# The first units of a hybrid encoder layer: adaLN columns and alpha/beta made in four 32-column groups of the array

## The chip, the core and the metric

The kernel runs on one core of one Trainium2 chip. A core has five instruction streams that run side by side and meet through semaphores: TensorE (matmul; PE in the profile, with its weight loads as PEld), VectorE (DVE), ScalarE (ACT), GpSimd (POOL) and SyncE (SP), the last of which here only issues transfers (DMA) between device memory and the core's own memory. The metric is the device time of one execution in microseconds (us); lower is better.

## The reference, cut to what matters

One layer on a sequence of 1024 rows of width 1024. What the change touches is the front of it: the modulation that all of the input norm hangs on, and eight of the columns of the combined input projection.

```python
cond = jax.nn.silu(c)
mod = (cond @ w_ada[l] + b_ada[l])[:, None, :]
sh1, sc1, gt1, sh2, sc2, gt2 = jnp.split(mod, N_MOD, axis=-1)
h = rmsnorm(x, norm1_g[l]) * (1.0 + sc1) + sh1
proj = h @ w_in[l]
qa, ka, va, qkvb, zb, bb, ab, ga, gb = jnp.split(proj, IN_SPLITS, axis=-1)
...
beta = jax.nn.sigmoid(b_raw.astype(jnp.float32))
g = -jnp.exp(a_log.astype(jnp.float32)) * jax.nn.softplus(
    a_raw.astype(jnp.float32) + dt_bias.astype(jnp.float32))
```

`bb` and `ab` (four heads each) are the eight columns that this text calls alpha/beta. Behind them come a gated DeltaNet on `qkvb`, a chunked attention, a merge, and a feed-forward part that takes the larger half of the time.

## The kernel before, in words

Activations lie transposed: 128 of the 1024 channels on the partitions, the 1024 rows of the sequence along them, so a 1024-wide operand is eight tiles (k = 0 to 7). The order of everything is written out by hand, one program for each engine; nothing is scheduled by a tool.

A dense unit `ds` makes 128 output columns of a projection. Each operand is split into a high and a low part (`act_hi`, `act_lo`, `w_hi`, `w_lo`), and `dense_k` (L1189) issues for one k three products of two halves of 512 rows each, six matmuls of 128x512 in the fast fp32r format, into the PSUM pair `ps[ds % 2]`. Plain fp32 matmuls are also used; each shows as two records.

The start of the layer, which is where the change lies, goes like this.

- SP loads the small vectors, the first adaLN weights (`load_ada(0)`), the eight row tiles of x (tile t >= 4 waits until tile t-4 is transposed, since four places are shared), `load_ada(1)`, the weights of unit 0 and unit 1, three small vectors, `load_ada(2)`, `load_ada(3)`, the weights of units 2 to 5. Then come two stores: `xT_d` (L631, the transposed x, 4 MB) and `ext_d` (L633, a table of eight rows of 384 numbers, each written 128 times, 1.5 MB), and then the weights of units 6 to 8, each when its place in `w_raw` is free.
- TensorE transposes x, and for each of four pieces n of the modulation (256 shift and 256 scale columns) runs `modulation(n)`: 12 matmuls of 128x128 for the last three k, and 4 on a sum that VectorE has made of the first five (`ada_sum`, five instructions of 128x512). `beat` is filler work. `units01(n)` runs units 0 and 1 together, two k at a time, as soon as the low part of each k is there.
- Unit 0 is the alpha/beta unit: 128 columns from `C_AB` on are multiplied, of which eight are used (L1786). Unit 1 is the first of the twelve convolution units.
- VectorE and ScalarE turn x into `act_hi` and `act_lo`, two k for each piece n, once `mod_mm` says that the piece's columns are in PSUM.

From unit 1 on, a convolution unit d goes: matmuls on TensorE; ScalarE copies `ps` into `est[d % 2]` (L1776) and splits the weights of unit d+2; VectorE makes `w_lo` of d+2, adds three shifted taps (L2268), ScalarE a tanh, VectorE the product (L2273, `est_ready`); GpSimd issues the store to `qkvb_d` (L1050). Two rules tie this chain together: unit d+2 may not write `ps[d % 2]` before `est_ready` of d, and the copy of unit d into `est[d % 2]` waits until the store of unit d-2 has landed (`est_stored`, in `evac_conv`). The first such wait is that of unit 3 on the store of unit 1.

## Time and profile before

| | |
|---|---|
| median of three runs | 1651.31 us (1647.7 to 1651.38) |
| the profiled execution | 1652.54 us |
| its span | 1649.9 us |
| TensorE busy | 1608.8 us, 98% of the span |
| VectorE, ScalarE, GpSimd busy | 927.8, 638.9, 266.0 us |
| first step of units 0 and 1 | 43.5 us |
| first step of unit 2 | 72.55 us |
| first step of unit 5 | 107.33 us |

The page of the profile shows how full each engine is over the whole span. It says little on a change to the first 70 us: there the instructions in order of time, with the idle time ahead of each and its releaser in square brackets, are what is read. A busy share that is near 100% only says that work taken off TensorE may shorten the span; whether it does is decided by the next wait that does not depend on TensorE.

### The profile page before, as it was taken

What the parts mean: (1) busy time and instruction counts of PE and PEld (TensorE: products, weight loads), DVE (VectorE), ACT (ScalarE), POOL (GpSimd) and SP (SyncE); (2) the same over time, 40 slices, a digit from 0 to 9 for tenths busy, and PEclk for the clock granted to TensorE, in tenths of its full rate; (3) what the DMA queues carried; (4) which work ended last, traced back from release to release, by engine and by line L of the source; (5) the groups of instructions that cost most, each with busy time, mean ns of one, the idle gap of its engine ahead of it and who ended that gap; (6) DMA issues with size and microseconds to landing.
All of it is one profiled execution on the core that took longest, in us unless ns stands there. A gap on an engine that the chain in (4) does not pass through costs nothing.

```text
span 1649.9 us, 24004 instructions
## 1 busy us (share of the span) xinstructions
PE 1608.8 (98%) x8235; PEld 1328.9 (81%) x8235; DVE 927.8 (56%) x1459; ACT 638.9 (39%) x1308; POOL 266.0 (16%) x283
## 2 busy tenths in 40 slices
PE   5999999999999999999899999999999999999998
PEld 5877878888878787878788877888888888888887
DVE  5867665445444444545553399866666666334424
ACT  4234456555534444444212235333333333332413
POOL 1016580111110101100000012322332220000000
PEclk9999999999999999999999999999999999999999
DMA  9835657655833333422546312222222223643412
GB/s 296 221 104 191 223 170 227 183 178 153 250 101 106 103 108 97 132 101 99 171 148 203 102 53 77 97 84 87 76 76 76 95 75 138 216 177 130 145 45 102
DMA packets 223652, 223.42 MB, mean 135 GB/s; under 512 B 18025, under 2 KB 189162, under 8 KB 223594
## 3 DMA queue, kind: packets, MB, share of 16 engines
q1 hardware_dynamic: 216618, 197.50, 38.0%
q0 software_dynamic: 6976, 25.17, 4.0%
q8 instruction: 33, 0.54, 0.1%
q14 instruction: 25, 0.20, 0.0%
HBM read 162.35 MB, written 60.29 MB: 135 GB/s over the span
## 4 chain that ended last, share of the span: by engine, by line
PE 81%; DVE 4%; DMA 1%; ACT 1%; issue 0%; DVEq 0%; SPq 0%; ACTq 0%
PE pm L1595 22%; PE pm L1609 15%; PE pd L1454 11%; PE ps L1194 11%; PE pm L1194 9%; PE sc L1407 2%; PE tT L1430 2%; PE tT L1419 2%; PE pm L1507 1%; PE gps L1344 1%; DMA gst<-z_d 1%; PE pm L1549 1%; PE gps L1357 1%; PE gps L1378 1%; PE gps L1371 1%; PE gps L1364 1%
## 5 line engine op out<-in xcount | busy, mean ns | idle before, releaser
L1194 PE MATMUL ps<-act_hi,w_hi 128*128 128x512 f32 x464 | 154.4, 414 | 5.3 <-DVE est L2273 2.8
L2167 DVE TENSOR_TENSOR w_lo<-w_raw,w_hi 128x1024 fp32r<-128x1024 f32 x61 | 78.6, 1289 | 125.1 <-ACT w_hi L1701 115.6
L1194 PE MATMUL ps<-act_lo,w_hi 128*128 128x512 f32 x464 | 143.7, 391 | 0.0
L1194 PE MATMUL ps<-act_hi,w_lo 128*128 128x512 f32 x464 | 143.4, 390 | 0.0
L1609 PE MATMUL pm<-act_hi,w_hi 128*128 128x512 f32 x352 | 137.2, 390 | 0.0
L1609 PE MATMUL pm<-act_hi,w_lo 128*128 128x512 f32 x352 | 137.0, 389 | 0.0
L1609 PE MATMUL pm<-act_lo,w_hi 128*128 128x512 f32 x352 | 136.9, 389 | 0.0
L1595 PE MATMUL pm<-act_hi,w_hi 128*128 128x512 f32 x320 | 124.5, 389 | 0.0
L1595 PE MATMUL pm<-act_lo,w_hi 128*128 128x512 f32 x320 | 124.5, 389 | 0.0
L1595 PE MATMUL pm<-act_hi,w_lo 128*128 128x512 f32 x320 | 124.5, 389 | 0.0
L1454 PE MATMUL pd<-act_hi,w_hi 128*128 128x512 f32 x256 | 111.3, 435 | 0.0
L1194 PEld LDWEIGHTS ps<-act_lo,w_hi 128*128 128x128 f32 x464 | 87.1, 188 | 19.1
L1194 PEld LDWEIGHTS ps<-act_hi,w_lo 128*128 128x128 f32 x464 | 87.1, 188 | 19.0
L1454 PE MATMUL pd<-act_hi,w_lo 128*128 128x512 f32 x256 | 101.0, 394 | 0.0
L1454 PE MATMUL pd<-act_lo,w_hi 128*128 128x512 f32 x256 | 100.3, 392 | 0.0
L1194 PEld LDWEIGHTS ps<-act_hi,w_hi 128*128 128x128 f32 x464 | 80.8, 189 | 21.4 <-issue 9.0
L1595 PE MATMUL pm<-t_hi,w_hi 128*128 128x512 f32 x240 | 93.6, 390 | 3.3 <-DVE tmp L2638 3.3
L2744 DVE TENSOR_TENSOR w_lo<-w_raw,w_hi 128x512 fp32r<-128x512 f32 x44 | 30.4, 692 | 117.0 <-ACT w_hi L2069 116.9
L1170 POOL TENSOR_TENSOR est<-w_raw 128x512 f32<-128x512 f32 x20 | 27.1, 1353 | 418.8 <-DVE w_lo L2618 227.7
L1595 PE MATMUL pm<-t_hi,w_lo 128*128 128x512 f32 x240 | 93.4, 389 | 0.0
L1595 PE MATMUL pm<-t_lo,w_hi 128*128 128x512 f32 x240 | 93.4, 389 | 0.0
L1701 ACT ACTIVATE w_hi<-w_raw 128x1024 fp32r<-128x1024 f32 x61 | 64.4, 1056 | 60.2 <-PE pm L1194 53.1
(367 smaller groups left out, 3452.4 us busy)
## 6 DMA issues: line engine op xcount, KB each, us to landing
w_raw<-in_w_in_dram SPq DMA_DIRECT2D x45, 512.0 KB, 5.6
w_raw<-in_w_ffn_in_dram SPq DMA_DIRECT2D x44, 512.0 KB, 3.7
h_raw<-h_d SPq DMA_DIRECT2D x36, 512.0 KB, 3.4
a_raw<-in_w_ada_dram SPq DMA_DIRECT2D x32, 512.0 KB, 4.5
w_raw<-in_w_ffn_out_dram SPq DMA_DIRECT2D x44, 256.0 KB, 3.7
h_d<-hid SPq DMA_DIRECT2D x21, 512.0 KB, 2.6
pk_d<-pk SPq DMA_DIRECT2D x8, 768.0 KB, 3.7
qkva_d<-est POOLq DMA_DIRECT2D x12, 512.0 KB, 6.3
```

Of the source, the lines that this page charges most:

```text
L1170: pool.tensor_tensor(s1, upw[:, 0:4], upw[:, 4:8], ALU.add).then_inc(mix_ready, 1)
L1194: ins = pe.matmul(dst[:, cols], wt[:, ds % 2, k, :], at[:, cols], start=(first and n == 0), stop=(last and n == 2))
L1344: ins = pe.matmul(hd(gps, h), gst[:, (0 if q == Q_QS else 4) + h, :], hd(St, h), start=True, stop=True)
L1407: ins = pe.matmul(score_cols(e, c0, c1), ast[rows, 0, j * P:(j + 1) * P], ast[rows, 1, k0 + c0:k0 + c1], start=True, stop=True)
L1419: ins = pe.transpose(tT[:, kt * P:(kt + 1) * P], Pm[:, e, kt * P:(kt + 1) * P], ident[:, :])
L1430: ins = pe.matmul(tT[rows, 0:P], V[:, j - nk_ + 1 + kt, rows], PT[:, e, kt * P:(kt + 1) * P], start=(kt == 0), stop=(kt == nk_ - 1))
L1454: ins = pe.matmul(pd[:, half(h)], wt[:, ds % 2, kk, :], at[:, kk, half(h)], start=(kk == 0 and n == 0), stop=(kk == KT - 1 and n == 2))
L1595: ins = pe.matmul(bank(n, o), wt[:, c, :], at, start=(c == 0 and x == 0), stop=(c == 3 and x == 2))
L1609: ins = pe.matmul(out_bank(b, h), wt[:, b, :], at[:, j % 8, half(h)], start=(t % NF == 0 and x == 0), stop=(t % NF == NF - 1 and x == 2))
L1701: act.activation(w_hi[:, ds % 2], w_raw[:, ds % NR], ACT.Copy).then_inc(whi_ready, 1)
L2167: dve.tensor_tensor(w_lo[:, ds % 2], w_raw[:, ds % NR], w_hi[:, ds % 2].bitcast(F32), ALU.subtract)\
L2744: dve.tensor_tensor(lo, w_raw[:, raw_o(t) % NR, 0:4], hi.bitcast(F32), ALU.subtract)\
```

## The change

Four things are changed, all in the first units.

1. The modulation pieces. `modulation(n)` and VectorE's `ada_sum(n)` go. `columns(n)` is eight fp32 matmuls of 32x512 on TensorE: the stationary operand is one column of silu(c) repeated 32 times, the moving operand a row block of the adaLN weights, and k goes to the 32-column group k % 4 of the array, that is to partitions 32(k % 4) and on of `aT`. ScalarE copies `aT` to `asum` (`copy_columns`), and `turn_columns(n)`, four matmuls of 128x128, adds the four groups through `sel[:, 0]`, which is 1 at partitions 0, 32, 64 and 96. `mod_mm` counts two for a piece now.
2. Alpha/beta. Unit 0 goes, and with it its weights' place in `w_raw`. 32 columns of `w_in` lie in a tile of their own, `wab`. `ab_block(k)`, at odd k, runs eight fp32 matmuls of 32x512: for two k, for `act_hi` and `act_lo`, for both halves; the four (k, operand) pairs go to the four groups. ScalarE copies all 128 partitions of `ps[0]`, and the transposes become products with `sel`, which add the groups.
3. The order. `columns(0)` stands between the transposes of x tiles 2 and 3, `turn_columns(0)` behind tile 5; SP loads `wab` and unit 1 ahead of `load_ada(1)`; ScalarE and VectorE split unit 1's weights before the first norm; unit 2's weights may be split without waiting for a unit.
4. GpSimd makes `sel` with three small additions.

```diff
+        sel = sb("sel", [P, 2 * B_H])
...
+            wab = sbin(st0, "wab", [P, KT, 32])
...
         ACT_X = (3, 6)
+        AB_COLS = 32
...
                 load_x(t)
+            sp.dma_start(wab[:, :, :], w_in_v[:, :, C_AB:C_AB + AB_COLS]).then_inc(misc_in, 16)
+            sp.sem_inc(raw_in[0], 16)
+            load_unit(1, 0, w_in_v, C_QKVB + group(1) * P)
             load_ada(1)
-            for d in range(2):
-                load_unit(d, 0, w_in_v, C_AB if d == 0 else C_QKVB + group(1) * P)
             sp.dma_start(rrow[:, :], rel_rev).then_inc(rel_in, 16)
...
+            pool.wait_ge(consts_ready, 3)
+            ch.link(pool.tensor_tensor(sel[:, :], ident[:, 0:8], ident[:, AB_COLS:AB_COLS + 8], ALU.add))
+            ch.link(pool.tensor_tensor(sel[:, :], sel[:, :], ident[:, 2 * AB_COLS:2 * AB_COLS + 8], ALU.add))
+            pool.tensor_tensor(sel[:, :], sel[:, :], ident[:, 3 * AB_COLS:3 * AB_COLS + 8], ALU.add)\
+                .then_inc(consts_ready, 1)
             for n, b in enumerate((BLK, 2 * BLK)):
...
-            def units01(n):
-                for d, k in in_step(2 * n, 2 * n + 2):
-                    if d == 0:
-                        pe.wait_ge(lo_ready, k + 1)
-                    ins = dense_k(d, k, ps[d], act_hi[:, k, :], act_lo[:, k, :], k == 0, k == 7)
-                    if k == 7:
-                        ins.then_inc(dense_mm, 1)
+            def ab_block(k):
+                if k == 1:
+                    pe.wait_ge(misc_in, 48)
+                for b in (k - 1, k):
+                    for x, at in enumerate((act_hi, act_lo)):
+                        for h in range(2):
+                            c = 2 * b + x
+                            rows = slice(c % 4 * AB_COLS, (c % 4 + 1) * AB_COLS)
+                            ins = pe.matmul(ps[0][rows, half(h)], wab[:, b, :], at[:, b, half(h)].bitcast(F32),
+                                            start=(c < 4), stop=(c >= 2 * KT - 4))
+                if k == KT - 1:
+                    ins.then_inc(dense_mm, 1)
+            def units01(k):
+                pe.wait_ge(lo_ready, k + 1)
+                if k % 2:
+                    ab_block(k)
+                ins = dense_k(1, k, ps[1], act_hi[:, k, :], act_lo[:, k, :], k == 0, k == KT - 1)
+                if k == KT - 1:
+                    ins.then_inc(dense_mm, 1)
...
+            def columns(n):
+                pe.wait_ge(ada_in[n], ada_count(n))
+                if n:
+                    pe.wait_ge(asum_ready, n)
+                for k in range(KT):
+                    ins = pe.matmul(aT[k % 4 * AB_COLS:(k % 4 + 1) * AB_COLS, :],
+                                    cs[:, k:k + 1].broadcast_to([P, AB_COLS]), ada_row(n, k),
+                                    start=(k < 4), stop=(k >= 4))
+                ins.then_inc(mod_mm, 1)
+            def turn_columns(n):
+                pe.wait_ge(asum_ready, n + 1)
+                if n:
+                    pe.wait_ge(mod_ready, n)
+                for q in range(4):
+                    ins = pe.matmul(gps[:, q * P:(q + 1) * P], asum[:, n % 2, q * P:(q + 1) * P],
+                                    sel[:, 0:1].broadcast_to([P, P]), start=True, stop=True)
+                ins.then_inc(mod_mm, 1)
...
-            def modulation(n):
...
-            pe.wait_ge(cs_ready, 1)
-            pe.wait_ge(vecT_ready, 2)
-            modulation(0)
-            beat(12)
+                if t == 2:
+                    pe.wait_ge(cs_ready, 1)
+                    columns(0)
+                if t == 5:
+                    pe.wait_ge(vecT_ready, 2)
+                    pe.wait_ge(consts_ready, 4)
+                    turn_columns(0)
+            beat(8)
             pe.wait_ge(diag_ready, 1)
...
             ins.then_inc(rb_mm, 1)
-            modulation(1)
+            columns(1)
+            turn_columns(1)
+            pe.wait_ge(xt_read, NT)
             beat(8)
-            pe.wait_ge(xt_read, NT)
             pe.wait_ge(wlo_ready, 2)
             units01(0)
-            modulation(2)
+            columns(2)
             units01(1)
-            modulation(3)
+            turn_columns(2)
             units01(2)
             units01(3)
+            columns(3)
+            units01(4)
+            turn_columns(3)
+            for k in (5, 6, 7):
+                units01(k)
             for d in range(2, D_CONV):
...
                     pe.wait_ge(mod_ready, 1)
+                    pe.wait_ge(consts_ready, 4)
                     for t in range(NT):
-                        ins = pe.transpose(gps[:, t * 8:(t + 1) * 8], est[0:8, 0, t * P:(t + 1) * P],
-                                           ident[0:8, 0:8])
+                        ins = pe.matmul(gps[:, t * 8:(t + 1) * 8], est[:, 0, t * P:(t + 1) * P], sel[:, :],
+                                        start=True, stop=True)
                     ins.then_inc(abT_mm, 1)
...
                 act.wait_ge(raw_in[ds % NR], raw_count(ds, i))
-                if ds >= 2:
+                if ds >= 3:
                     act.wait_ge(dense_mm, ds - 1 + 4 * i)
...
             act.activation(ngh[:, :], vT[:, V_NG:V_NG + 1], ACT.Copy, scale=0.5).then_inc(act_chain, 1)
+            def copy_columns(n):
+                act.wait_ge(mod_mm, 2 * n + 1)
+                act.activation(asum[:, n % 2, :], aT[:, :], ACT.Copy).then_inc(asum_ready, 1)
             for t in range(NT):
+                if t == 5:
+                    copy_columns(0)
                 act.wait_ge(xr_in[t % 4], 16 * (t // 4 + 1))
...
                                    ACT.Copy).then_inc(xt_read, 1)
-            act.wait_ge(misc_in, 32)
+            act.sem_inc(whi_ready, 1)
+            split_hi(1)
+            act.wait_ge(misc_in, 48)
             act.activation(negA[:, :], negA[:, :], ACT.Exp).then_inc(act_chain, 1)
-            for n in range(4):
-                for k in (2 * n, 2 * n + 1):
-                    act.wait_ge(xn_ready, k + 1)
-                    act.activation(act_hi[:, k, :], est[:, k % 2, :], ACT.Identity,
-                                   bias=modT[:, SH1 + k:SH1 + k + 1]).then_inc(hi_ready, 1)
-                    if n == 0:
-                        split_hi(k)
+            copy_columns(1)
+            for k in range(KT):
+                if k == 3:
+                    copy_columns(2)
+                if k == 5:
+                    copy_columns(3)
+                act.wait_ge(xn_ready, k + 1)
+                act.activation(act_hi[:, k, :], est[:, k % 2, :], ACT.Identity,
+                               bias=modT[:, SH1 + k:SH1 + k + 1]).then_inc(hi_ready, 1)
...
                     act.wait_ge(lo_ready, KT)
-                    act.activation(est[0:8, 0, :], ps[0][0:8, :], ACT.Copy).then_inc(ab_read, 1)
+                    act.wait_ge(dense_mm, 1)
+                    act.activation(est[:, 0, :], ps[0][:, :], ACT.Copy).then_inc(ab_read, 1)
                     continue
...
-            def ada_sum(n):
...
-            ada_sum(0)
             for t in range(NT):
...
             dve.wait_ge(xt_read, NT)
-            ada_sum(1)
+            dve.wait_ge(whi_ready, 1)
+            dve.sem_inc(wlo_ready, 1)
+            split_lo(1)
...
             for n in range(4):
-                if n in (1, 2):
-                    ada_sum(n + 1)
-                dve.wait_ge(mod_mm, n + 1)
+                dve.wait_ge(mod_mm, 2 * n + 2)
                 two = slice(2 * n, 2 * n + 2)
...
                     norm_scale(k, xT0[:, k, :], gs[:, k:k + 1], aS[:, :], 0)
-                if n == 0:
-                    split_lo(0)
-                    split_lo(1)
                 for k in (2 * n, 2 * n + 1):
...
                     dve.wait_ge(abT_mm, 1)
-                    dve.wait_ge(misc_in, 32)
+                    dve.wait_ge(misc_in, 48)
                     ch.link(dve.tensor_copy(ab[:, :, :], gps[:, 0:64].rearrange("p (t h) -> p t h", t=NT)))
...
```

On TensorE the first steps of the units change most. Before, with the buffers' numbers (`ps0` is unit 0, `ps1` unit 1), the first k, in which unit 0 comes ahead of unit 1:

```order
L1194 MATMUL ps0<-act_hi,w_hi 128x512 [waits lo_ready,wlo_ready,xt_read]
L1194 MATMUL ps0<-act_hi,w_hi 128x512
L1194 MATMUL ps0<-act_lo,w_hi 128x512 x2
L1194 MATMUL ps0<-act_hi,w_lo 128x512 x2
L1194 MATMUL ps1<-act_hi,w_hi 128x512 x2
```

and now, from the same place on, up to the end of the second k:

```order
L1203 MATMUL ps1<-act_hi,w_hi 128x512 [waits lo_ready,wlo_ready]
L1203 MATMUL ps1<-act_hi,w_hi 128x512
L1203 MATMUL ps1<-act_lo,w_hi 128x512 x2
L1203 MATMUL ps1<-act_hi,w_lo 128x512 x2
L1259 MATMUL aT<-ada_raw,cs 32x512 [waits asum_ready,ada_in2]
L1259 MATMUL aT<-ada_raw,cs 32x512 x7
L1234 MATMUL ps0<-act_hi,wab 32x512 [waits misc_in,lo_ready]
L1234 MATMUL ps0<-act_hi,wab 32x512
L1234 MATMUL ps0<-act_lo,wab 32x512 x2
L1234 MATMUL ps0<-act_hi,wab 32x512 x2
L1234 MATMUL ps0<-act_lo,wab 32x512 x2
```

Unit 0's six matmuls of each k have become eight of 32x512 for every two k, and the piece's columns stand behind the first k.

On ScalarE, from the last square of x on (`tmp,ss<-xr`) to the copy of alpha/beta, before:

```order
L1713 ACTIVATE tmp,ss<-xr 128x1024 [waits ss_ready,xr_in3]
L1721 ACTIVATE negA<-negA 128x4 [waits misc_in]
L1725 ACTIVATE act_hi<-est,modT 128x1024 [waits xn_ready]
L1701 ACTIVATE w_hi<-w_raw 128x1024 [waits raw_in0]
L1725 ACTIVATE act_hi<-est,modT 128x1024 [waits xn_ready]
L1701 ACTIVATE w_hi<-w_raw 128x1024 [waits raw_in1]
L1725 ACTIVATE act_hi<-est,modT 128x1024 [waits xn_ready] x6
L1701 ACTIVATE w_hi<-w_raw 128x1024 [waits dense_mm,raw_in2]
L1786 ACTIVATE est<-ps 8x1024 [waits lo_ready]
```

and now:

```order
L1762 ACTIVATE tmp,ss<-xr 128x1024 [waits ss_ready,xr_in3]
L1743 ACTIVATE w_hi<-w_raw 128x1024 [waits raw_in1]
L1772 ACTIVATE negA<-negA 128x4 [waits misc_in]
L1754 ACTIVATE asum<-aT 128x512 [waits mod_mm]
L1780 ACTIVATE act_hi<-est,modT 128x1024 [waits xn_ready] x3
L1754 ACTIVATE asum<-aT 128x512 [waits mod_mm]
L1780 ACTIVATE act_hi<-est,modT 128x1024 [waits xn_ready] x2
L1754 ACTIVATE asum<-aT 128x512 [waits mod_mm]
L1780 ACTIVATE act_hi<-est,modT 128x1024 [waits xn_ready] x3
L1743 ACTIVATE w_hi<-w_raw 128x1024 [waits raw_in2]
L1840 ACTIVATE est<-ps 128x1024 [waits dense_mm,lo_ready]
```

Three copies of `aT` stand between the `act_hi` now (the first, of piece 0, stands ahead of the square of tile 5), and unit 2's weights wait for no unit.

On SyncE the transfers from the late x tiles on, before:

```order
L580 DMA xr<-in_x_dram 128x1024 [waits xt_mm,ss_ready] x4
L586 DMA adab<-in_w_ada_dram 128x8x256 x2
L566 DMA w_raw<-in_w_in_dram 128x8x128 x2
L596 DMA rrow<-in_rel_table_dram 8x257
L597 DMA negA<-in_a_log_dram 128x4
```

and now:

```order
L583 DMA xr<-in_x_dram 128x1024 [waits xt_mm,ss_ready] x4
L596 DMA wab<-in_w_in_dram 128x8x32
L569 DMA w_raw<-in_w_in_dram 128x8x128
L589 DMA adab<-in_w_ada_dram 128x8x256 x2
L600 DMA rrow<-in_rel_table_dram 8x257
```

A quarter of one unit's bytes has taken the place of that unit, and what follows down to `ext_d` and units 6 to 8 is as it was.

## Rows read from the trace of the kernel before

**Rows 1.** Timeline, TensorE: start us, us, engine, line, operation, tiles, shapes, count [idle before].
```profile
43.52 0.47 PE L1194 MATMUL ps<-act_hi,w_hi 128*128 128x512 f32 x1 [2.49 <-DVE act_lo L2217]
...
49.05 0.83 PE L1247 MATMUL gps<-cs,ada_raw 128*128 128x128 f32 x6
...
52.54 0.71 PE L1194 MATMUL ps<-act_hi,w_hi 128*128 128x512 f32 x2
...
72.55 0.64 PE L1194 MATMUL ps<-act_hi,w_hi 128*128 128x512 f32 x2
...
105.62 0.61 PE L1194 MATMUL ps<-act_hi,w_lo 128*128 128x512 f32 x2
107.33 0.70 PE L1194 MATMUL ps<-act_hi,w_hi 128*128 128x512 f32 x2 [1.10 <-DVE est L2273]
```

**Rows 2.** Timeline, ScalarE and VectorE, unit 3's evacuation and its last step.
```profile
97.69 1.12 ACT L1776 ACTIVATE est<-ps,wcT 128x1024 f32<-128x1024 f32 x1 [5.21 <-DMA qkvb_d<-est]
...
105.96 1.22 DVE L2273 SCALAR_TENSOR_TENSOR est<-tmp,est 128x1024 f32<-128x1024 f32 x1 [1.13 <-ACT tmp L1780]
```

**Rows 3.** Timeline, the queues of SP and POOL: when transfers are issued.
```profile
14.84 4.53 SPq L580 DMA_DIRECT2D xr<-in_x_dram  x4
...
48.37 1.74 SPq L631 DMA_DIRECT2D xT_d<-xT  x1
50.15 1.78 SPq L633 DMA_DIRECT2D ext_d<-ext  x1
...
82.56 0.77 POOL L1050 DMA_DIRECT2D qkvb_d<-est  x1 [47.16 <-DVE est L2273]
```

**Rows 4.** The tile qkvb_d, window 82 to 84: unit 1's store.
```profile
DMA to landing us min/median/max: 15.0/15.0/15.0
```

**Rows 5.** DMA queues in 82.5:86, 86:93.5, 94:98: packets, MB, share of 16 engines.
```profile
q0 software_dynamic: 72, 0.26, 18.3%
...
q1 hardware_dynamic: 762, 0.62, 57.6%
...
q0 software_dynamic: 154, 0.57, 43.2%
```

**Rows 6.** Stretches: us, TensorE busy (instructions), granted clock, DMA share, GB/s.
```profile
31.00:49.00 18.00, 14.60 (x104) 1.00 1.09 321
55.00:62.00 7.00, 7.00 (x49) 1.00 1.02 422
65.00:72.00 7.00, 7.00 (x32) 1.00 0.45 48
...
792.50:796.00 3.50, 3.23 (x8) 0.51 0.90 321
```

**Rows 7.** Timeline, TensorE, 128x64 products in two column groups; first row from window 467.36:467.50.
```profile
467.37 0.33 PE L1430 MATMUL tT<-PT,V 128*64 128x128 f32 x2
...
519.15 1.31 PE L1430 MATMUL tT<-PT,V 128*64 128x128 f32 x20
520.40 0.50 PE L1454 MATMUL pd<-act_hi,w_hi 128*128 128x512 f32 x1
```

**Rows 8.** Timeline, TensorE, windows 122.4:122.89 and 122.89:122.92: an fp32 matmul's two records.
```profile
122.47 0.59 PE L1293 MATMUL aT<-gm,after 128*128 128x512 f32 x1
...
122.47 1.02 PE L1293 MATMUL aT<-gm,after 128*128 128x512 f32 x2
```

**Rows 9.** Timeline, TensorE, behind long idle times, and the same transposes later.
```profile
12.79 1.97 PE L1234 MATMUL ps<-ident,xr 128*128 128x128 f32 x8 [7.86 <-DMA xr<-in_x_dram]
...
22.60 1.09 PE L1234 MATMUL ps<-ident,xr 128*128 128x128 f32 x8 [0.73 <-DMA xr<-in_x_dram]
...
792.77 1.22 PE L1194 MATMUL pm<-y_hi,w_hi 128*128 128x512 f32 x2 [4.37 <-DVE y_lo L2464]
```

**Rows 10.** Waits of TensorE up to 145 us: total, times, longest.
```profile
PE gps L1293 <- DVE pk L2260: 1.1, 1, 1.1
PE gps L1293 <- POOL gm L1060: 0.9, 1, 0.9
```

More of the change, by code:

```diff
@@ L1227, in _, with beat @@
             pe.transpose(gps[:, 0:n], vrow[:, :], ident[0:n, 0:n]).then_inc(vecT_mm, 1)
+            def columns(n):
[15 more added lines that the diff above has]
+                ins.then_inc(mod_mm, 1)
+            def beat(count):
+                for _ in range(count):
+                    pe.matmul(aT[:, 0:P], ones[:, :], ident[:, :], start=True, stop=True)
             for t in range(NT):
@@ L1236, in _ @@
                 ins.then_inc(xt_mm, 1)
-            def modulation(n):
-                pe.wait_ge(ada_in[n], ada_count(n))
-                pe.wait_ge(asum_ready, n + 1)
-                if n:
-                    pe.wait_ge(mod_ready, n)
-                for q in range(4):
-                    dst = gps[:, q * P:(q + 1) * P]
-                    for k in range(5, KT):
-                        pe.matmul(dst, ada_row(n, k)[:, q * P:(q + 1) * P], cs[:, k:k + 1].broadcast_to([P, P]),
-                                  start=(k == 5), stop=False)
-                    ins = pe.matmul(dst, asum[:, n % 2, q * P:(q + 1) * P], ones[:, :], start=False, stop=True)
-                ins.then_inc(mod_mm, 1)
-            def beat(count):
-                for _ in range(count):
-                    pe.matmul(aT[:, 0:P], ones[:, :], ident[:, :], start=True, stop=True)
-            pe.wait_ge(cs_ready, 1)
-            pe.wait_ge(vecT_ready, 2)
-            modulation(0)
-            beat(12)
+                if t == 2:
[6 more added lines that the diff above has]
+            beat(8)
             pe.wait_ge(diag_ready, 1)
@@ L2180, in evac_x @@
                     .then_inc(xt_read, 1)
-            def ada_sum(n):
-                dve.wait_ge(ada_in[n], ada_count(n))
-                dst = asum[:, n % 2, :]
-                ch.link(dve.tensor_scalar(dst, ada_row(n, 0), cs[:, 0:1], None, ALU.mult))
-                for k in range(1, 5):
-                    ins = dve.scalar_tensor_tensor(dst, ada_row(n, k), cs[:, k:k + 1], dst, ALU.mult, ALU.add)
-                    if k < 4:
-                        ch.link(ins)
-                ins.then_inc(asum_ready, 1)
-            ada_sum(0)
             for t in range(NT):
```

## Prediction, made before the changed kernel was run

> **What bounds the kernel now.** I read TensorE's instructions in order of time first. It waits 2.49 us for the first `act_lo`, starts the units at 43.52, runs through to 105.62 (and some 0.45 more for the last pair), and idles 1.1 us until unit 5 starts at 107.33 [rows 1]. So between 43.5 and 106.1 TensorE is the bound: work taken off it moves everything up to there.
>
> Then I asked what holds unit 5. It needs unit 3's last step on VectorE, which starts at 105.96 and takes 1.22; that chain begins at 97.69 with ScalarE's copy of unit 3, which sat 5.21 us waiting for a transfer, the store of unit 1 [rows 2]. It was issued at 82.56 [rows 3] and landed 15.0 us later [rows 4]. From 97.69 to 107.33 runs a chain of 9.64 us (copy, split, three taps, tanh, product) that does not contain TensorE.
>
> Why did 0.5 MB take 15 us? The transfers are full up to the big store of x, at 1.09 and 1.02 of the engines' time; then, from 65 on, the share is 0.45 at 48 GB/s: this is `ext_d`, issued at 50.15 behind `xT_d` [rows 3, 6]. 1.5 MB at 48 GB/s are 32 us, from about 63 to 95. Of unit 1's store, 72 packets moved before 86, none from 86 to 93.5 (only q1 is listed there), and the rest after 94 [rows 5]. So the store ended because `ext_d` ended. The clock that starts unit 5 is the transfer queue, not TensorE, and TensorE is only 1.25 us early against it today.
>
> **The change part by part.**
>
> *The array groups.* A plain fp32 matmul is two records; at 512 columns the second starts 0.43 us behind the first [rows 8], where one record is listed up to 122.89 and two from there. If four column groups run side by side, eight such matmuls (16 records) take 4 x 0.43 = 1.72 us; one after another 16 x 0.43 = 6.9. The trace has two groups, not four: of the 128x64 products two records lie in the same 0.14 us at 467.37, with one duration of 0.33, and 20 records take 520.40 - 519.15 = 1.25 us [rows 7]. A 128x128 record alone costs 0.109 (a modulation, 32 records, takes 52.54 - 49.05 = 3.49 [rows 1]), so twenty in a row would be 2.18 and ten pairs 1.09. Two groups do run in parallel, with some 0.16 for entering and leaving. I take 1.72 + 0.2 = 1.9 for each block of eight, `columns` or `ab_block`; the ends are 1.7 and 6.9.
>
> By the Trainium skill (TensorE: Matmul & The Clock Gate, Part 3: Packing small matmuls) packed matmuls start and end strictly in program order. By that rule a pair in one group would hold back the next group; in rows 7 two neighbours in different groups start at once, which the order of a matmul's two records does not allow if both halves of the first come first. The rule is the third rival below.
>
> *TensorE between its first unit step and unit 2.* Now: 29.03 us (43.52 to 72.55) = 16 steps of 1.38 (24 pairs in 5.53 us up to 49.05 are four steps) and two modulations of 3.49 [rows 1]. After: 8 steps x 1.38 = 11.0; four `ab_block` and two `columns`, 6 x 1.9 = 11.4; two `turn_columns`, each four of the sixteen matmuls of a modulation, 2 x 0.87 = 1.7. Sum 24.1: 4.9 us less. The first step comes some 3 to 4 us earlier, since the sum of piece 1 leaves VectorE's way to the first norm, though `columns(0)` now holds up the transposes of x tile 3 by 1.9. Against it stands a new wait: `act_hi(5)` is queued on ScalarE behind the copy of piece 3, which waits for `columns(3)`, and `turn_columns(3)` stands ahead of k = 5 on TensorE; I allow 2 us. Unit 2 then starts at 72.55 - 4.9 - 3.5 + 2 = 66.2. Its weights no longer wait for a unit, and the copy of `ps[0]` is queued in front of nothing that is late. Units 2 to 4 take 33.5 as now, plus 0.6 because the eight `sel` products load 128 columns instead of 8. TensorE is done with unit 4 at 100.3 instead of 106.1: 5.8 us gained.
>
> *Off VectorE.* The four sums and one weight split go, the split of unit 1 moves ahead. VectorE is not the bound after 68, so this is worth only what it did for the start above.
>
> *What the gain meets.* Unit 5 still waits for `est_ready` of unit 3, at 107.3. TensorE idles about 7 us there in place of 1.25. The 5.8 us end in this wait. What counts is whether `ext_d` ends earlier. Two terms. First, SP moves 128 KB instead of 512 KB ahead of it: at 321 GB/s [rows 6] 0.38 MB is 1.2 us; if the small pieces of `wab` cost as much each as the larger ones, nothing. Between 0 and -1.2 I take -0.6. Second, x tile 7 may only be issued when tile 3 is transposed, now behind `columns(0)`: up to 1.9 later, in a queue that has tiles 5 and 6 in front of it (four x tiles from 14.84 on) [rows 3]. Between 0 and +1.9 I take +0.4. Sum -0.2 us, ends -1.2 and +1.9.
>
> *The clock.* Behind 4.37 us of idle TensorE the granted clock was 0.51 for 3.5 us, the 1.2 GHz level, and 792.77's pair took 1.22; behind 7.86 us the transposes took 1.97 for eight against 1.09 [rows 6, 9]. Seven idle us ahead of unit 5 will do the same: 3.5 to 5 us at half rate, 1.7 to 2.5 us lost in unit 5. Of that, the next two waits of TensorE take back 0.9 (for GpSimd's gates, made behind unit 4's store) and 1.1 (for VectorE's `pk`) [rows 10]: both hang on chains that start at unit 3's last step, on VectorE and GpSimd. I take all of it as absorbed; the bound is +0.7.
>
> *Sum.* -0.2 + 0 = -0.2 us. Against the profiled execution's 1652.54 that is 1652.3; against the median of 1651.31, 1651.1, and the latter is what I forecast, rounded to 1651.0. Its own range is -1.5 to +2.6 and the spread of the runs (3.7 us): 1647.5 to 1654.5.
>
> **The rivals.**
>
> 1. *The store of unit 1 does not hang on `ext_d` but takes its 15 us from the issue.* For it: its two halves landed on different engines, and the same chain would then move with TensorE. Against: nothing moved from 86 to 93.5. Unit 5 would start when TensorE is free, at 100.3: -7.0, 1644.3. By the Trainium skill (DMA: Bandwidth & Descriptors, Queues, rings and completion order) an engine takes turns between its queues packet by packet, which speaks for this rival; the trace shows the software queue standing still beside the other, so I give it little.
>
> 2. *The groups do not run side by side when there are four, or in fp32 with 32 columns.* Then the first unit steps cost 6.9 in seven blocks (four `ab_block`, `columns(1)` to `(3)`): 7 x 5.0 = +35, less the 7.0 of idle before unit 5 and the 2.0 behind it: +26, 1677. Rows 7 speak against it.
>
> 3. *Slower, from the order of starts.* In `ab_block` a group gets both halves of the sequence, four records, before the next group. If starts keep to program order, each next group begins with the last record of the one before: 13 x 0.43 = 5.6 instead of 1.72, and `columns`, two records per group, 9 x 0.43 = 3.9. That is 4 x 3.9 + 3 x 2.2 = 22 us more on TensorE; 7.0 of it lies in the idle time, 2.0 in the two waits behind: +13, 1664. It decides from about 1.2 us of excess per block on (7.0 over six blocks); below that the cover holds and the time is as forecast. The 128x64 products can't show it fully: they alternate groups after each matmul.
>
> 4. *The clock is not given back,* or x tile 7 delays the whole queue: +1.5 to +3, 1653 to 1654. This stays within the likeliest case's own range.
>
> **How the numbers follow.** A measurement of this kernel tells 0.3%, about 5 us, from no change. Forecast with rival 4: 0.82, all of it "same". Rival 1: 0.07, faster by more than 5. Rivals 2 and 3: 0.03 and 0.06, slower. Odds and ends beyond 5 us on the fast side 0.02. So faster 0.09, same 0.82, slower 0.09. The range has to hold eight in ten: 1646 to 1656 leaves out rivals 1, 2 and 3, together 0.16.
>
> **What would show it.** In the changed profile: (a) `columns` and `ab_block` at under 2.2 us each, with four records starting together; (b) unit 2 starting at 64 to 69; (c) ScalarE's copy of unit 3 waiting for `qkvb_d<-est` for more than 10 us, until 96 to 99, and the 48 GB/s stretch ending at 93 to 96 as now; (d) TensorE idle some 7 us ahead of unit 5, which starts at 106.5 to 109, with the granted clock at half behind it; (e) from 137 on all instructions within 2 us of where they are now. It is wrong if unit 5 starts before 104, because the store lands early, or after 111, because the blocks take over 3 us.

## The result: slower, and the profile after

| | before | changed |
|---|---|---|
| median | 1651.17 us (4 runs) | 1662.99 us (4 runs, 1661.9 to 1664.16) |
| ratio | | 1.0071, 95% interval [1.0059, 1.0083] |
| span of the profiled execution | 1649.9 us | 1661.3 us |

Every median here is over the fast executions of a kernel, which leaves out one, of 5713 us (the kernel with `t` moved by 32 bytes, below).

The change costs 11.4 us of span. The forecast was no change, 1651.0 in a range of 1646 to 1656, so it was wrong, and by a loss that none of its rivals had the mechanism of.

The front is not where it went. Here is TensorE in order of time in the changed kernel, to be read against [rows 1] (start us, us, engine, line, operation, tiles, shapes, count, idle before):

```profile
40.38 1.92 PE L1259 MATMUL aT<-ada_raw,cs 128*32 128x512 f32 x16
42.12 0.59 PE L1234 MATMUL ps<-act_hi,wab 128*32 128x512 f32 x1
42.12 0.62 PE L1234 MATMUL ps<-act_lo,wab 128*32 128x512 f32 x1
42.14 0.62 PE L1234 MATMUL ps<-act_hi,wab 128*32 128x512 f32 x1
42.15 0.62 PE L1234 MATMUL ps<-act_lo,wab 128*32 128x512 f32 x1
42.55 0.59 PE L1234 MATMUL ps<-act_hi,wab 128*32 128x512 f32 x1
...
43.98 0.50 PE L1203 MATMUL ps<-act_hi,w_hi 128*128 128x512 f32 x1
...
65.38 0.62 PE L1203 MATMUL ps<-act_hi,w_hi 128*128 128x512 f32 x2
...
99.43 0.61 PE L1203 MATMUL ps<-act_hi,w_lo 128*128 128x512 f32 x2
105.77 1.19 PE L1203 MATMUL ps<-act_hi,w_hi 128*128 128x512 f32 x2 [5.72 <-DVE est L2312]
106.76 1.05 PE L1203 MATMUL ps<-act_lo,w_hi 128*128 128x512 f32 x2
107.61 1.05 PE L1203 MATMUL ps<-act_hi,w_lo 128*128 128x512 f32 x2
...
111.02 0.76 PE L1203 MATMUL ps<-act_hi,w_hi 128*128 128x512 f32 x2
```

Four records start within 0.03 us and the next four 0.43 us later: the groups run side by side. A block of eight takes 43.98 - 42.12 = 1.86 us. Unit 2 starts at 65.38, TensorE is done with unit 4 at 100.0, and unit 5 then waits 5.7 us.

The wait is the one that the prediction names. The store of unit 1 is issued 7.2 us earlier than in [rows 3] and lands only 1.6 us earlier (at 96.0, not 97.6), and ScalarE's copy of unit 3 waits for it longer than in [rows 2] (GpSimd's queue, landing of that store, ScalarE):

```profile
75.39 0.77 POOL L1059 DMA_DIRECT2D qkvb_d<-est  x1 [41.66 <-DVE est L2312]
```

```profile
DMA to landing us min/median/max: 20.6/20.6/20.6
```

```profile
96.12 1.12 ACT L1829 ACTIVATE est<-ps,wcT 128x1024 f32<-128x1024 f32 x1 [9.72 <-DMA qkvb_d<-est]
```

Now the same matmuls, from the end of the program back, compared by their start in both kernels. The table is worked out from the start times of both traces:

| us in the kernel before | 137 | 413 | 797 | 865 | 1022 | 1396 | 1600 | end |
|---|---|---|---|---|---|---|---|---|
| changed minus before, us | -1.5 | -0.1 | -0.3 | +1.9 | +1.3 | +8.3 | +11.0 | +11.4 |

Up to 797 us nothing is lost. The whole loss comes after it, in code that the diff does not touch and without a wait: 2.2 us from 797 to 865, where TensorE multiplies `y` with `w_hi`, nothing from 865 to 1022, where it is mostly `act` with `w_hi`, and the rest from 1022 on. The stretches show it (us, TensorE busy with its instructions, PEld, DVE, ACT, POOL, granted clock, DMA share, GB/s); first the kernel before, then the changed one:

```profile
800.00:865.00 65.00, 65.00 (x289) 53.72 (x288) 40.23 (x35) 13.67 (x13) 0.00 (x0) 1.00 0.46 156
1070.00:1396.00 326.00, 326.00 (x1440) 269.95 (x1439) 220.11 (x310) 112.10 (x190) 81.85 (x60) 1.00 0.26 86
1400.00:1600.00 200.00, 200.00 (x884) 165.62 (x883) 74.82 (x81) 62.71 (x78) 0.00 (x0) 1.00 0.43 152
```

```profile
800.00:865.00 65.00, 65.00 (x281) 52.20 (x280) 39.57 (x33) 12.72 (x13) 0.00 (x0) 1.00 0.45 147
1070.00:1396.00 326.00, 326.00 (x1412) 264.82 (x1411) 213.59 (x304) 108.74 (x186) 81.92 (x60) 1.00 0.26 84
1400.00:1600.00 200.00, 200.00 (x872) 163.50 (x871) 77.70 (x85) 62.46 (x78) 0.00 (x0) 1.00 0.45 157
```

TensorE is busy throughout and the clock is full, but fewer matmuls go through: 1412 instead of 1440 in 326 us, 326 us / 1412 = 230.9 ns each instead of 226.4.

### The profile page after: what moved, and what is told of

It reads as the page before. It is cut to its first block, busy times and chain, and to the rows that moved or that the text cites. A ratio compares the mean times of both kernels' runs of the same rounds, so it can differ in the third digit from the quotient of the medians.

```text
span 1661.3 us, 23963 instructions
## 1 busy us (share of the span) xinstructions
PE 1619.2 (97%) x8219; PEld 1315.3 (79%) x8219; DVE 908.8 (55%) x1438; ACT 639.6 (39%) x1311; POOL 267.9 (16%) x286
## 4 chain that ended last, share of the span: by engine, by line
PE 86%; DVE 4%; DMA 4%; POOL 2%; issue 1%; ACT 1%; SPq 1%; DVEq 0%; POOLq 0%; ACTq 0%
PE pm L1637 21%; PE pm L1651 15%; PE ps L1203 13%; PE pd L1496 11%; PE pm L1203 9%; PE sc L1449 2%; PE tT L1472 2%; PE pm L1591 2%; PE tT L1461 2%; POOL Xi L1119 1%; PE pm L1549 1%; DMA qkvb_d<-est 1%; POOL pr L1117 1%; PE gps L1386 1%; DMA gst<-z_d 1%
## 5 line engine op out<-in xcount | busy, mean ns | idle before, releaser
L1203 PE MATMUL ps<-act_hi,w_hi 128*128 128x512 f32 x448 | 151.0, 418 | 7.8 <-DVE est L2312 7.3
L2221 DVE TENSOR_TENSOR w_lo<-w_raw,w_hi 128x1024 fp32r<-128x1024 f32 x60 | 74.2, 1236 | 128.3 <-ACT w_hi L1743 117.4
L1203 PE MATMUL ps<-act_hi,w_lo 128*128 128x512 f32 x448 | 139.9, 393 | 0.0
L1203 PE MATMUL ps<-act_lo,w_hi 128*128 128x512 f32 x448 | 139.8, 393 | 0.0
L1179 POOL TENSOR_TENSOR est<-w_raw 128x512 f32<-128x512 f32 x20 | 26.7, 1335 | 426.1 <-DVE w_lo L2657 233.5
L2045 ACT ACTIVATE w_hi<-w_raw 128x512 fp32r<-128x512 f32 x80 | 50.1, 630 | 96.1 <-PE pm L1637 96.1
```

The source lines that it names most:

```text
L1179: pool.tensor_tensor(s1, upw[:, 0:4], upw[:, 4:8], ALU.add).then_inc(mix_ready, 1)
L1203: ins = pe.matmul(dst[:, cols], wt[:, ds % 2, k, :], at[:, cols], start=(first and n == 0), stop=(last and n == 2))
L2045: act.activation(op_slot(o)[0], op_source(n, o), ACT.Copy).then_inc(whi_ready, 1)
L2221: dve.tensor_tensor(w_lo[:, ds % 2], w_raw[:, ds % NR], w_hi[:, ds % 2].bitcast(F32), ALU.subtract)\
```

## Theories for the 11 us

The diff has one line that reaches so far: `sel = sb("sel", ...)`, 32 bytes on each partition, is allocated ahead of most other tiles. `act_hi`, `act_lo`, `w_hi`, `w_lo` lie in front of it and stay. `y_hi`, `y_lo`, `t_hi`, `t_lo`, `w3_hi`, `w3_lo` and all other later tiles move by 32 bytes. In the kernel before, all these operands start at 128 modulo 256 (`act_hi` 16512, `w_hi` 98432, `y_hi` 132992, `t_hi` 165760, `w3_hi` 214912).

*Place*: the late matmuls are slower because of where their operands lie. *Front*: the new front carries through (its transfers, idle time, clock). *Move*: any new layout is slower.

**Four kernels on the addresses.**

```diff
 # e1_after_pad32, the changed kernel
         sel = sb("sel", [P, 2 * B_H])
+        pad = sb("pad", [P, 8])
 # e2_before_pad32, the kernel before
         after = sb("after", [P, P])
+        pad = sb("pad", [P, 8])
 # e3_before_pad64, the kernel before
+        pad = sb("pad", [P, 16])
 # e4_after_sel_late, the changed kernel
-        sel = sb("sel", [P, 2 * B_H])
...
             ext = sbin(st0, "ext", [A_H, EXT])
+            sel = sbin(st0, "sel", [P, 2 * B_H])
```

> The changed kernel with 32 more bytes per partition behind the new tile sel, so that every tile allocated behind it lies 64 bytes (not 32) from where it lay in the kernel before. Theory P (place): the 11.4 us come from operands of the late matmuls (y_hi, y_lo, t_hi, t_lo, w3_hi, w3_lo) that lie 32 bytes off a 64-byte boundary, and nothing from the new front. Then they go, and the time is that of the kernel before less the 1.3 us by which unit 5 and the start of the chain run ahead, minus what is absorbed: 1649.5 to 1651.5, and 512-column matmuls that read y_hi or t_hi start every 226.7 ns again. Theory F (front): the late stages are slower because of what the new front does (its DMA order, the idle time and the clock). Then nothing changes: 1662 to 1664. Theory M (any move): what counts is that tiles have moved at all. Then 1658 to 1664.

> The kernel before with an unused tile of 32 bytes per partition where the changed kernel has sel, and no other edit. Theory P: all of the loss without any of the change, 1651.2 + 11.5 = 1662.7 (1661 to 1664), with 512-column matmuls on y_hi at 233 ns and on t_hi at 232 ns from start to start. Theory F: 1651. Theory M: 1658 to 1664.

> The kernel before with an unused tile of 64 bytes per partition in the same place. Theory P: 1651.2 as before, since all operands lie on a 64-byte boundary; if the boundary that counts is one of 128 bytes, it is slow like the pad of 32. Theory M: slow, 1658 to 1664. Theory F: 1651, as for the pad of 32 (this run alone does not tell F from P).

> The changed kernel with sel allocated as the last tile of the first scope, whose room is given up before the late stages: every tile that is not in that scope has the address that it has in the kernel before. Theory P: as for the changed kernel with the 32 bytes more, 1649.5 to 1651.5. Theory F: 1662 to 1664. It differs from the first run of this call if a shift by 64 bytes also costs something (then this one alone is back at 1650 to 1651).

The ratios are the record's; they are not the quotients of the two medians.

| | median us | ratio to before (1650.02) |
|---|---|---|
| changed, 64 bytes in all | 1661.43 | 1.0068 [1.0052, 1.0083] |
| before, unused 32 bytes | 1664.05 | 1.0085 [1.0066, 1.0104] |
| before, unused 64 bytes | 1657.65 | 1.0054 [1.0037, 1.0071] |
| changed, `sel` in the first scope | 1651.98 | 1.0006 [0.9996, 1.0016] |

Thirty-two unused bytes cost all of it without any of the change, and the whole change without the move costs nothing. *Front* is dead. The stretches of the last kernel are back at the old count:

```profile
1070.00:1396.00 326.00, 326.00 (x1440) 270.04 (x1439) 220.49 (x312) 112.36 (x190) 81.83 (x60) 1.00 0.26 86
```

My bet on a 64-byte boundary was wrong: 64 bytes cost 9 us too (8.8 and 8.6 us from 797 to 1600 by the starts of the two traces).

**What has to agree with what.** In the changed kernel the seven products of the feed-forward loop differ. Products 0 and 1 multiply moved weights (`w3`) with unmoved `act`: 233 ns. Products 5 and 6, unmoved `w_hi` with moved `t`: 233.5. Product 2, moved `w3` with moved `t`, settles at 227 after five matmuls. That suggests that the two operands of a matmul must agree with each other, not with a boundary.

```diff
 # r1_all_operands_32, the kernel before
+        pad = sb("pad", [P, 8])
         with ExitStack() as st:
             ada_raw = sbin(st, "ada_raw", [P, 2, KT, S])
         act_hi = sb("act_hi", [P, KT, S], F32R)
 # dw3_only_w3_32, the kernel before
+            sbin(st3, "pad", [P, 8])
             w3_hi = sbin(st3, "w3_hi", [P, 3, 4, P], F32R)
 # dt_only_t_32, the kernel before
+            sbin(st3, "pad", [P, 8])
             t_hi = sbin(st3, "t_hi", [P, 3, 4, HALF], F32R)
...
+            sbin(st3, "pad2", [P, 24])
             w3_hi = sbin(st3, "w3_hi", [P, 3, 4, P], F32R)
 # m128_t_and_w3_128: one pad of 32 numbers ahead of t_hi; m256_t_and_w3_256: of 64
```

> The kernel before with an unused tile of 32 bytes per partition ahead of act_hi, so that every tile, weights and moving operands alike, lies 32 bytes further and none against another. Theory R (relative): a matmul is slow where its moving operand and its weights begin at different offsets within 128 bytes. In the changed kernel the products with weights in w3 and moving tiles in act start every 233 ns, those with weights in w_hi and moving tiles in t every 233.5 ns, but the one with both in moved tiles (w3 and t_hi) settles at 227 ns after five matmuls. Then this kernel has the time of the one before, 1649 to 1652. Theory A (absolute): a matmul is slow where an operand lies off a 128-byte boundary. Then every 512-column fp32r matmul goes from 227 to 233 ns or more, the 6500 or so of them add 6 ns each, and the time is 1685 to 1695.

> The kernel before with 32 unused bytes ahead of w3_hi, so that only w3_hi and w3_lo (the weights of three of the seven products, and of steps t % 7 = 0, 1, 2 of the last stage) lie 32 bytes off. Both theories: products 0 and 1 (240 matmuls each, 6.3 ns more) 3.0 us, the 456 matmuls of the last stage at 233 instead of 226.8 ns 2.8 us, products 3 to 6 unchanged at 226.7. They part at product 2, whose moving operand t_hi has not been moved here: R says that it is now slow too, 233 ns instead of the 229.3 it had in the changed kernel, 1.5 us, and the time is 1650.5 + 7.3 = 1658 (1656 to 1659). If its time is that of the changed kernel or less, R is wrong.

> The kernel before with 32 unused bytes ahead of t_hi and 96 ahead of w3_hi: t_hi and t_lo lie 32 bytes off, w3_hi and w3_lo 128 bytes further, which is no move within 128 bytes. R and A: products 5 and 6 (t against w_hi) at 233.5 ns as in the changed kernel, 3.2 us; products 0 and 1 and the last stage at 226.7, although w3 has moved by 128. Product 2 (t against w3) at 233, 1.5 us. Time 1650.5 + 4.7 = 1655 (1653.5 to 1656.5). If it is any move at all that costs, products 0, 1 and the last stage stay slow and it is over 1659.

> The kernel before with 128 unused bytes ahead of t_hi: t_hi, t_lo, w3_hi and w3_lo all lie 128 bytes further, nothing else. The last call said that a move of w3 by 128 bytes against act is slow too (product 0 and 1 at 233 ns), so what counts is at least the offset within 256 bytes. Theory R256 (slow where moving operand and weights begin at different offsets within 256 bytes): products 0 and 1 (w3 against act), 5 and 6 (t against w_hi) and steps 0 to 2 of the last stage at 233 ns, product 2 (both moved by 128) near 227 after its first five matmuls as in the changed kernel: 1650.5 + 9 = 1659.5 (1658 to 1661). Theory A128 is dead by this: it says 1650.5.

> The same with 256 bytes. R256: a move by 256 changes no offset within 256, so 1650.5 (1649 to 1652) and 226.7 ns everywhere. If a larger period counts (512 or more), it is slow like the move by 128, 1658 to 1661; against that speaks that in the kernel before w_hi (address 98432, 128 within 512) is used against t_hi (165760, 384 within 512) at full pace. If any move costs: also 1658 to 1661.

| moved against the kernel before | median us | ratio |
|---|---|---|
| everything by 32 bytes | 1650.44 (before 1651.75) | 0.9994 [0.9984, 1.0005] |
| `w3` by 32 | 1657.68 (1651.75) | 1.0042 [1.0025, 1.0059] |
| `t` by 32, `w3` by 128 | 1663.36 (1651.75) | 1.0082 [1.0062, 1.0103] |
| `t` and `w3` by 128 | 1661.8 (1652.13) | 1.0047 [1.0031, 1.0062] |
| `t` and `w3` by 256 | 1650.52 (1652.13) | 0.9991 [0.9982, 1.0000] |

The mean time from start to start, worked out from the starts in each trace (ns; 240 matmuls for each product; the last column is the last stage's steps with `w3` weights):

| product: weights, moving | 0, 1: w3, act | 2: w3, t | 3: w_hi, act | 4: w_hi, act | 5, 6: w_hi, t | last stage |
|---|---|---|---|---|---|---|
| before | 226.7 | 226.7 | 226.7 | 226.7 | 226.8 | 226.8 |
| changed (`t`, `w3` by 32) | 233.1 | 229.3 | 228.7 | 226.7 | 233.5 | 232.9 |
| everything by 32 | 226.7 | 226.7 | 226.7 | 226.7 | 226.7 | 226.8 |
| `w3` by 32 | 233.1 | 233.4 | 227.0 | 226.7 | 227.1 | 232.8 |
| `t` by 32, `w3` by 128 | 233.3 | 234.1 | 230.4 | 226.7 | 233.4 | 232.2 |
| `t` and `w3` by 128 | 233.2 | 228.6 | 227.0 | 226.7 | 233.0 | 232.3 |
| `t` and `w3` by 256 | 226.7 | 226.7 | 226.7 | 226.7 | 226.8 | 226.8 |

Moving everything is free: by the expectation above, an absolute boundary would have cost 35 us and more. *Move* falls with it, and with the last row. Moving one operand of a pair is slow at 32, 64 and 128 bytes and free at 256 (products 5 and 6 take 229 to 230 ns at 64, products 0 and 1 take 233); product 2 of `t` by 32, `w3` by 128, whose operands differ by 96, takes 234.1. Steps between, such as 192 bytes, were not tried. Moving both by the same amount is free but for the first matmuls. Product 3 of the changed kernel has only unmoved operands, and its first five matmuls still take 228 to 236 ns, although product 2 had settled at 226.7 from its sixth to its last but one. So going from a pair at one common offset to a pair at another costs a few matmuls too.

My expectation for `t` by 32 took 128 bytes for a whole period and was 8 us low; that miss gave the period. The next two kernels bear it out, the one at 128 bytes with 1661.8 where 1658 to 1661 was expected. Why the offset counts is not settled: the trace shows the pace, not the port.

## Where the gain of the front went

With the tiles in place the change gives 1650.9 to 1652.0 in three measurements, as predicted, though TensorE is done with unit 4 earlier than before, by 4.4 us in two of the three traces and 2.5 in the third (6.1 in the changed kernel). Two things were said to hold it: the store of unit 1 ends with `ext_d`, and the clock halves behind the wait. Each was taken away. The first edit stores the eight rows once, and copies them 128-fold from device memory later, behind the load of unit 6 (65.5 instead of 50.1 us).

```diff
 # x1_ext_16_engines (sel in the first scope), x2_before_ext_16 (the kernel before)
-                    sp.dma_start(ext_d.rearrange("h (p n) -> h p n", n=EXT),
-                                 ext[:, :].unsqueeze(1).broadcast_to([A_H, P, EXT])).then_inc(ext_stored, 16)
+                    sp.dma_start(ext_s, ext[:, :]).then_inc(ext_stored, 16)
+                if d == 6:
+                    sp.wait_ge(ext_stored, 16)
+                    sp.dma_start(ext_d.rearrange("h (p n) -> p h n", n=EXT),
+                                 bass.AP(ext_s.tensor, 0, [[0, P], [EXT, A_H], [1, EXT]])).then_inc(ext_stored, 16)
```

> The changed kernel with its tiles in place (sel in the first scope), and with the 1.5 MB of ext_d made in two steps: 12 KB of ext to a small tensor, then one broadcast from there with the 128 rows as its outer dimension, behind the load of unit 6. Theory S (the store of unit 1 stands behind ext_d, as the prediction has it): its store lands by 86 to 88 instead of 96, unit 5 starts when TensorE is done with unit 4, at 100 to 101 instead of 105.8, the granted clock does not halve, and 5.5 + 3 us are gained at 120. How much of it reaches the end was never seen: small gains at 120 (1 us) came through to the end, losses of 3 to 4 us by half. All of it: 1651.5 - 8.5 = 1643; half of it: 1647. Rival: unit 5 waits for something else than that store (est of unit 3 on VectorE, a load); then it starts at 105 as now, and the time is 1650 to 1652.

> The kernel before with the same two steps for ext_d. Theory S: TensorE comes out of unit 4 only at 106.1 there, and waits 1.1 us for est; so no more than that 1.1 us can be gained, 1649.5 to 1651. The gain of the new front (5.8 us at 100) is then to be had only with both edits: this run near 1650 and the one with both at 1643 to 1647. If this run gains as much as that one, the gain is of the transfer (other loads land earlier), not of the TensorE time saved.

With the new front 1646.25 us (1644.19 to 1646.38), ratio 0.9956 [0.9943, 0.9969]; with the old front 1650.82, ratio 0.9989 [0.9980, 0.9998]. Both as expected. The first is faster than both kernels. Its ScalarE:

```profile
91.51 1.12 ACT L1833 ACTIVATE est<-ps,wcT 128x1024 f32<-128x1024 f32 x1 [2.80 <-PE ps L1207]
```

Then the stretch behind the wait, in the changed kernel and in this one:

```profile
105.00:110.00 5.00, 4.23 (x10) 3.39 (x11) 4.49 (x18) 2.06 (x2) 0.53 (x1) 0.50 0.26 105
```

```profile
105.00:110.00 5.00, 5.00 (x24) 4.14 (x23) 4.51 (x4) 0.38 (x1) 0.00 (x0) 1.00 0.00 0
```

The copy of unit 3 now waits for TensorE, not for a transfer, and the clock is full where it was half. Its starts lie 6.2 us ahead of the kernel before at 137 us and 5.2 at the end. On the two forms of the transfer, the changed kernel first, then this one:

```profile
79.00:86.00 7.00, 7.00 (x32) 5.79 (x31) 4.98 (x4) 1.88 (x3) 0.00 (x0) 1.00 0.47 52
```

```profile
65.00:72.00 7.00, 7.00 (x37) 4.92 (x30) 2.02 (x3) 3.09 (x3) 0.00 (x0) 1.00 0.86 284
```

The old form held a share near 0.5 at some 50 GB/s. In the new row two weight loads run beside the copy. By the Trainium skill (DMA: Bandwidth & Descriptors, Why a DMA increments its semaphore by 16 and not by 1) a transfer is split over the largest number of engines, 16 at most, that divides the slowest dimension of both its sides: eight for eight rows, all for 128. The shares, 0.47 and 0.86, agree. The edit also changes the source and the place in the queue, and no run separates these from the number of engines; what it does show is that without the long transfer unit 1's store lands after 3.3 us and unit 5 doesn't wait.

**Filling the wait.** These three and their comparison ask what the half clock costs.

```diff
 # x4_beats_at_unit5 (sel in the first scope); x5_22_beats: beat(22)
+            beat(40)
             for d in range(D_CONV, D_A):
 # x3_beats_before_unit5: in the loop of units 2 to 4, which d == 5 never reaches
+                if d == 5:
+                    beat(40)
```

> The changed kernel with its tiles in place, and 40 matmuls of 128x128 fp32 without use (0.12 us each by the eleven that take 1.39 us at 38.78) in the 5.7 us in which TensorE waits ahead of unit 5. The wait for est stays, so unit 5 begins at 105.8 as before. Theory C (the time lost behind the wait is that of the half clock): the granted clock stays at 1.0 behind 105, the 3.4 us (6.8 us at half) are not lost, 120.2 comes 3 to 3.5 us earlier than in the kernel without them, and the time goes from 1652.0 to 1649 (1648 to 1650.5), since such early gains have come through to the end. Theory D (what is late behind the wait is the chain of stores and loads, not TensorE's pace): the clock stays but unit 6 waits longer, and the time is 1651.5 to 1652.5.

> The changed kernel with its tiles in place and 40 matmuls of 128x128 fp32 without use (0.12 us each, 5 us) between unit 4 and unit 5, in front of the wait for est. In the last call these stood in a loop that never reaches unit 5, so that run was the kernel without them a second time. Theory C: the granted clock stays at 1.0 behind 105, unit 5 still starts when est is there, the 3.4 us of the half clock are not lost, 120.2 comes about 3 us earlier against the start of unit 5, and the time goes from 1651.6 (the two runs without them) to 1648.5 (1647.5 to 1650). Theory D (unit 6 and what follows wait longer instead, the chain of stores is what is late): 1651 to 1652.5.

> As the last run with 22 instead of 40 matmuls without use. The last trace has 80 records in 9.09 us for 40 of them, so one takes 0.227 us (not 0.12) and the 40 held unit 5 up until 110.7, and its time still was 1649.8 against 1652.0 and 1651.2 without any. 22 take 5.0 us and end at about 105.5, before est comes. Theory C: unit 5 starts with est (105.8), clock 1.0, 120.2 comes 3 us earlier than without them, and the time is 2 to 3.5 us below that of the kernel without them in the same call: 1648.5 (1647 to 1650). Theory D: within 1 us of it.

> The changed kernel with its tiles in place and nothing else, for the third time, beside the one with 22 matmuls without use on the same chip: 1651.5 (1650.5 to 1652.5).

The first, 1651.21 us, ratio 1.0002 [0.9989, 1.0014], issued nothing new and only repeats the kernel with `sel` in the first scope. The second, 1649.8 us, ratio 0.9993 [0.9983, 1.0002], was mis-sized: I had read eleven records as eleven matmuls, and an fp32 matmul has two; it held unit 5 up until 110.71. The third, 1646.04 us, ratio 0.9979 [0.9968, 0.9991], against 1650.87, ratio 1.0008 [0.9996, 1.0019], for the same kernel without it. TensorE with the 22, and then its comparison:

```profile
99.80 5.07 PE L1277 MATMUL aT<-ident,ones 128*128 128x128 f32 x44
105.45 0.70 PE L1203 MATMUL ps<-act_hi,w_hi 128*128 128x512 f32 x2 [0.58 <-DVE est L2313]
105.99 0.62 PE L1203 MATMUL ps<-act_lo,w_hi 128*128 128x512 f32 x2
```

```profile
106.78 1.19 PE L1203 MATMUL ps<-act_hi,w_hi 128*128 128x512 f32 x2 [5.09 <-DVE est L2312]
107.77 1.05 PE L1203 MATMUL ps<-act_lo,w_hi 128*128 128x512 f32 x2
108.62 1.05 PE L1203 MATMUL ps<-act_hi,w_lo 128*128 128x512 f32 x2
```

The pair takes 0.62 where it took 1.05. So the filler keeps the clock full, and the time of the kernel is lower. But the traces do not show that the one brings the other. This table, worked out from them, has how much later than in the kernel before things happen: the end of unit 3's last step (`est_ready`), the start of unit 5, and the matmuls that the kernel before starts at 112, 120 and 137 us:

| us later than before | `est_ready` of unit 3 | unit 5 | at 112 | at 120 | at 137 |
|---|---|---|---|---|---|
| changed | -1.6 | -1.6 | +1.0 | -0.1 | -1.5 |
| the same with its tiles in place (e4b_again) | -0.6 | -0.6 | +0.9 | -0.2 | -0.5 |
| that and 22 filler matmuls | -1.9 | -1.9 | -1.9 | -1.9 | -1.9 |
| tiles in place and `ext_d` in two steps, no filler | -6.2 | -5.1 | -5.3 | -6.2 | -6.2 |

The half clock costs 2.6 and 1.5 us up to 112, and all of it is regained by 137, in the two waits that the prediction names. With 22 they are as long as in [rows 10]; in the changed kernel the only wait of TensorE from 105 to 145 us is the one for `est`:

```profile
PE gps L1335 <- DVE pk L2300: 1.1, 1, 1.1
PE gps L1335 <- POOL gm L1069: 1.0, 1, 1.0
```

In sixteen of the seventeen traces TensorE at 137 is as late or early as `est_ready` of unit 3, to 0.3 us; the other is the kernel with 40, whose filler held unit 5 up. So up to 137 the filler gains nothing. The 1.3 us by which this execution with 22 leads its comparison at 137 are there before the filler starts: unit 1's store landed at 95.7 and not 97.0, and in kernels with the long transfer the landing varies from 95.1 to 100.7.

The medians still differ by 4.8 us. Most of it is, in the traces, at 790, where the next long wait was short this time, 1.93 instead of 4.37 us in [rows 9], and the clock behind it stayed full:

```profile
788.66 0.73 PE L1203 MATMUL pm<-y_hi,w_hi 128*128 128x512 f32 x2 [1.93 <-DVE y_lo L2504]
```

From 787 to 797 us this trace gains 3.4 us on its comparison. The wait is 1.7 to 4.7 us long in the seventeen traces. It is short in both kernels with filler (1.9 and 2.3) and in one of the fifteen without (1.7, the kernel before with 64 unused bytes); the others have 2.9 or more. What makes it short is left open, and so is how the filler would reach it.

## Why the prediction was wrong, point by point

- *Bound and chain* (TensorE to 106, then the store behind `ext_d`): right. With `ext_d` out of the way unit 5 does not wait.
- *The array groups*, 1.9 us a block: right, 1.86 for `ab_block` and 42.12 - 40.38 = 1.74 for `columns`. Rivals 2 and 3 are refuted by four starts in 0.03 us.
- *Unit 2 at 66.2, unit 4 done at 100.3*: 65.38 and 100.0.
- *Rival 1* (the store takes 15 us from its issue): refuted, it took 20.6 and landed at 96.0.
- *The clock*, 1.7 to 2.5 us lost in unit 5 and all of it absorbed: right. Six pairs took 111.02 - 105.77 = 5.25 us instead of 2.8, some 2.4 us, and by 137 TensorE was again as far ahead (1.5 us) as at the start of unit 5 (1.6).
- *Sum of the front*, -0.2: with the tiles in place the ratio is 1.0006 [0.9996, 1.0016], 1.0002 [0.9989, 1.0014] and 1.0008 [0.9996, 1.0019], 0 to +1 us. Right within its range. The term itself was too fine to be tested: in the five traces with the new front, the old transfer and no filler unit 5 starts anywhere from 105.8 to 110.4.
- *Slips that change nothing*: "24 pairs in 5.53 us" are 24 matmuls, and the low end of the sum's range, -1.5, is -1.2 by its own terms.
- *The step that failed* is (e), "from 137 on all instructions within 2 us". It holds to 797 and fails behind. The part-by-part account priced what every edit does and not where it puts things: `sel` was read as 128 columns of weight load, its 32 bytes of room as nothing. The missing term: about 2.2 us from 797 to 865 (`y` against `w_hi`), 7.0 from 1022 to 1396 and 2.7 to 1600. The forecast plus this term is 1662.9; measured were 1662.99. That they agree so closely is luck: three executions of one and the same kernel, the changed one with its tiles in place, end 0.7 us before to 3.1 us behind the kernel before.

## What to carry to other kernels

A new tile is an edit to every tile allocated behind it. Ahead of a forecast, list the start addresses of all matmul operands before and after, and look whether weights and moving operand of each pair still start at the same offset modulo 256 bytes; put small tiles last or in a scope that is given up. Where time is saved on an engine ahead of a wait for a transfer, the saving is worth nothing until the transfer is sped up too: here 1652.0 became 1646.3. A stretch at half clock costs nothing where the waits behind it give the time back; look at those before filling the gap.

## What the runs showed of the hardware that I had not expected

- Streams of 128x512 fp32r matmuls run at 226.7 ns from start to start where both operands start at the same offset modulo 256 bytes, and at 232 to 234 ns where they differ by 32 or 128; by 64, at 229 to 233. That is up to 3% of such a matmul's time. Where a pair at one common offset follows a pair at another, the first few are slow too (five at 32 bytes).
- Four 128x32 fp32 groups run fully in parallel, though in `ab_block` four records of a group stand ahead of the next group in the program: eight matmuls in 1.74 to 1.86 us. The Trainium skill (TensorE: Matmul & The Clock Gate, Part 3: Packing small matmuls) has starts in strict program order. The measurement differs: four groups' first records start within 0.03 us, and no cost of such an order shows.
- A transfer whose outer dimension is 8 moved at some 50 GB/s, and another queue's store beside it took 20.6 us; with the same bytes copied from device memory with an outer dimension of 128, and done before the store was issued, it landed in 3.3 us.
